# A decoder layer on one core: the order of the expert loads of a lane, and the sums of the conv norm moved to VectorE

## The chip, the cores and the metric

The kernel runs on one core of one Trainium2 chip. The metric is the device time of one execution in microseconds (us). A difference counts from about 0.5% of it, some 4.4 us.

## What is computed

One decoder layer for 512 tokens of width 1024, in 32-bit floats. The first half mixes tokens, the second half sends each token to two of 16 experts:

```python
h = _modulate(_rmsnorm(x, norm_mix_g[l]), sh1, sc1)
proj = h @ w_in                       # 1024 x 7168: q, fz, i, og, ca, cb, gate_a, gate_b
o = _hgrn2_chunkwise(q, k, v, log_f)  # 8 heads
y_a = (_rmsnorm(o, onorm_g) * silu(og)) @ w_o_hgrn
u = conv(ca * sigmoid(cb)) + conv_b   # 512 channels, 31 taps
u = jax.nn.silu(_layernorm(u, ln_g, ln_b))     # over the 512 channels
y_b = u @ w_o_conv
x = x + g1 * ((sigmoid(gate_a) * y_a + sigmoid(gate_b) * y_b) @ w_out)
for e in range(N_EXPERTS):            # group-limited top 2
    a = silu(hf @ w_gate[e]) * (hf @ w_up[e])
    y = y + comb[:, e:e + 1] * (a @ w_down[e])
```

## The kernel before

**Mixer.** `plan()` lists the weight chunks of 1 MB in the order in which TensorE uses them: cb, ca, then for each half of the heads (qd = 0, 1) fz, q, iv, og, then gb, yb, pairs of ga and ya, and wo. Each chunk has two tiles of output (yb: four), and tiles are numbered 0 to 79. A tile is 24 matmuls (yb: 12), since each 32-bit product is made of three (`mm3`, L555 to L557) from operands split into a high and a low part. The high part `w_hi` of a chunk is made by ScalarE (L939), the low part `w_lo` by VectorE (L1183), for chunk 24 by GpSimd (L1758, `POOL_SPLITS`); SyncE loads chunk n when the low part of chunk n-2 is done (L478). All engines walk the same list of tiles; between the tiles they do what `SLOT` puts behind a tile, each engine its own part, in program order.

Around the change these are tiles 40 to 47 (gb, evacuated by ScalarE into `mb`), 48 to 55 (yb, chunks 24 and 25, evacuated by VectorE) and 56 on (ga, ya). Behind tiles 40 to 44 come the last five steps x1 to x5 of the HGRN branch: transposes, state updates, outputs, mean squares (L700) and the spread of their inverse roots (L706, which waits for the reciprocal L1402 of VectorE). Then VectorE norms the heads (`o_norm`, L1432), GpSimd multiplies each with its gate (L1789), ScalarE and VectorE split it (L1029, L1437).

**Conv norm.** The conv has its result `acc` (4 channel tiles of 128 x 512) before tile 40. Its norm is four steps `("ln", 0..3)`, behind tiles 40 to 43. In step 0 TensorE forms the mean over the channels (L716, four matmuls of true 32-bit operands with `mean_c`), VectorE subtracts it (L1405), ScalarE squares (L1057). In step 1 TensorE forms the mean of the squares, again four matmuls, ScalarE takes the root (L1061), VectorE the reciprocal (L1410) and four products (L1413). In step 2 ScalarE makes the sigmoid (L1065), VectorE gain and bias (L1417) and the product (L1421). In step 3 ScalarE writes `cs_hi` (L1073) and VectorE `cs_lo` (L1425). Tile 48 is the first that reads them. After `cs_lo` GpSimd sets `ada_acc` to zero (L1792, at tile 44); SyncE waits for that between the loads of chunks 25 and 26 to load a bias row into it (L495). Loads of `ada_p` by ScalarE's queue and sums by VectorE (L1451, `ada_half`) follow from tile 50 on.

**Router.** VectorE makes the table of jobs. A job is 64 tokens of one expert; there are 24 jobs here. Three lanes (0, 1, 2) each have buffers for one expert, six pieces of 1 MB: 0 and 1 gate, 2 and 3 up, 4 and 5 down. Job j runs in round r = j // 3, lane j % 3. `jobs_i` says which expert a lane has in a round. The routing of these inputs gives lane 0 the experts 0 5 5 6 6 6 7 7, lane 1 15 down to 8, lane 2 1 1 2 3 4 4 4 4 in rounds 0 to 7: 13 of the 21 entries of rounds 1 to 7 need a load, 8 keep the expert.

**Expert loop.** For a job TensorE does in order: gate (pieces 0, 1; L856), the transposes of the job before (L878), up (2, 3; L856), the tokens of the next job (L846), down of the job before (4, 5; L892). Tokens come by a gather (GpSimd, L1805), results go by a scatter (L1816). SyncE refills the lanes; per round:

```python
for s, cs in ((0, (0, 1, 2, 3)), (1, (0, 1, 2, 3)), (0, (4, 5)), (2, (0, 1, 2, 3)), (1, (4, 5)), (2, (4, 5))):
    with sp.If(now[s] == old[s]):
```

Before each piece it waits until TensorE has released it. For a kept expert it loads 16 numbers in place of the piece, so that the count of the piece's semaphore goes on.

Of the kernel before, what the change touches and what calls it, by code (L numbers as in the profile page):

```python
# [92 lines left out]
def trunk_kernel(nc, xT, x, cols, consts, masks, w_ada, b_ada_row, w_in, w_o_hgrn, w_o_conv,  # L93
# [15 lines left out]
    with ctx:  # L109
# [177 lines left out]
        s_cz = sem("conv_silu_done")  # L287
        s_l1 = sem("ln_pe")
# [109 lines left out]
        for n in range(4):  # L398
            place(40 + n, ("ln", n))
# [66 lines left out]
        def _(sp):  # L466
# [60 lines left out]

            with sp.Fori(1, last + 1) as r:
                now = [sp.value_load(jobs_i[0:1, bass.ds(r + MAXR * s, 1)], min_val=0, max_val=NE - 1) for s in range(LANES)]
                old = [sp.value_load(jobs_i[0:1, bass.ds(r + (MAXR * s - 1), 1)], min_val=0, max_val=NE - 1) for s in range(LANES)]  # L530

                for s, cs in ((0, (0, 1, 2, 3)), (1, (0, 1, 2, 3)), (0, (4, 5)), (2, (0, 1, 2, 3)), (1, (4, 5)), (2, (4, 5))):
                    with sp.If(now[s] == old[s]):
                        for c in cs:
                            sp.wait_ge(s_gt if c < 2 else s_up if c < 4 else s_dn, r * LANES + (s - LANES + 1))
                            expert_load(sp, now[s], s, c, 16)
                    with sp.Else():
                        for c in cs:
                            sp.wait_ge(s_gt if c < 2 else s_up if c < 4 else s_dn, r * LANES + (s - LANES + 1))
                            expert_load(sp, now[s], s, c)  # L540
# [11 lines left out]
        def _(pe):  # L552
# [179 lines left out]
            for s, (kind, tile, n, t) in enumerate(steps):  # L732
# [148 lines left out]
            def down(j, r, s, first=False):  # L881
# [3 lines left out]
                for c in (4, 5):  # L885
                    pe.wait_ge(s_er[s][c], r * 16 + 16)
# [1004 lines left out]
```

## Time and profile before

| | us |
|---|---|
| median of 3 runs | 884.56 (883.62 to 887.65) |
| the profiled execution | 884.96 |
| its span, first to last instruction | 883.1 |
| TensorE busy | 819.2 |
| VectorE busy | 474.3 |
| ScalarE busy | 202.1 |
| GpSimd busy | 142.8 |

The granted clock of TensorE is the share of its full 2.4 GHz; it was 0.981 in the mean. A line such as L716 is a line of the kernel before. An idle time in brackets names what ended it. In the timelines consecutive instructions of one line stand in one row with their count.

### The profile page before, as it was taken

The numbers are of one execution on the slowest core, as the hardware profiler recorded it, in microseconds if no ns is written. First come the engines' busy times: TensorE is split into PE (matmuls) and PEld (weight loads), VectorE is DVE, ScalarE is ACT, GpSimd is POOL, SyncE is SP. The second block draws the span as 40 slices with busy tenths as digits, with TensorE's granted clock in tenths as the row PEclk, the third lists the DMA queues.
The fourth block names the chain that finished last, engine by engine and source line by source line (L and its number), as shares of the span: only waits on it lengthen the run. The fifth ranks groups of instructions, "written<-read, shape, count | busy, mean of one in ns | idle before, by whom it ended". The sixth has DMA issues, their size and how long they took to land.

```text
span 883.1 us, 14349 instructions
## 1 busy us (share of the span) xinstructions
PE 819.2 (93%) x5760; PEld 597.9 (68%) x5760; DVE 474.3 (54%) x634; ACT 202.1 (23%) x261; POOL 142.8 (16%) x200
## 2 busy tenths in 40 slices
PE   2999999999999999999999999799999889999960
PEld 0578889888799878778888898555555445555530
DVE  3659997995789956878777364611111101111117
ACT  3442211223321136412222523110000000000012
POOL 0000312220413200600000000022222212222220
PEclk9999999999999999999999999999999999999995
DMA  9922221212121211467774949996999999899316
GB/s 317 369 68 95 95 96 50 95 50 95 48 96 50 97 48 48 142 208 249 243 245 152 354 147 392 383 388 241 360 398 392 400 387 401 307 393 334 134 34 276
DMA packets 102303, 191.59 MB, mean 217 GB/s; under 512 B 4247, under 2 KB 41383, under 8 KB 102257
## 3 DMA queue, kind: packets, MB, share of 16 engines
q1 hardware_dynamic: 89138, 160.79, 50.4%
q10 hardware_dynamic: 9168, 19.40, 6.5%
q0 software_dynamic: 3952, 10.76, 3.3%
q8 instruction: 33, 0.54, 0.3%
q14 instruction: 12, 0.10, 0.0%
HBM read 182.55 MB, written 10.49 MB: 219 GB/s over the span
## 4 chain that ended last, share of the span: by engine, by line
PE 81%; DVE 7%; DMA 4%; SPq 4%; issue 2%; ACT 2%; POOL 0%; ACTq 0%; DVEq 0%; POOLq 0%
PE proj L856 16%; PE proj L555 15%; PE proj L557 14%; PE proj L556 14%; PE ha L892 8%; SPq L456 3%; PE pp L661 2%; PE pp L846 1%; DMA ew<-in_w_gate 1%; DMA xt_t<-in_xT 1%; PE ha L569 1%; PE ha L878 1%; PE ha L691 1%; PE pp L639 1%; PE pp L716 1%
## 5 line engine op out<-in xcount | busy, mean ns | idle before, releaser
L856 PE MATMUL proj<-ew,heT 128*64 128x256 f32 x1536 | 177.0, 383 | 5.9 <-DMA ew<-in_w_gate 3.8
L856 PEld LDWEIGHTS proj<-ew,heT 128*64 128x64 f32 x1536 | 109.5, 138 | 72.0 <-issue 17.8
L555 PE MATMUL proj<-h_hi,w_hi 128*128 128x512 f32 x368 | 146.2, 397 | 3.5 <-DVE h_lo L1224 3.0
L557 PE MATMUL proj<-h_hi,w_lo 128*128 128x512 f32 x368 | 143.4, 390 | 0.0
L556 PE MATMUL proj<-h_lo,w_hi 128*128 128x512 f32 x368 | 143.4, 390 | 0.0
L1346 DVE SCALAR_TENSOR_TENSOR acc<-u_t,cols_t,acc 128x512 f32<-128x512 f32 x120 | 91.1, 807 | 0.6
L892 PE MATMUL ha<-ew,aT 128*64 128x512 f32 x384 | 87.9, 599 | 1.8 <-DVE aT L1693 0.9
L1183 DVE TENSOR_TENSOR w_lo<-w_raw,w_hi 128x2048 fp32r<-128x2048 f32 x35 | 80.2, 2290 | 15.7 <-ACT w_hi L939 15.7
L939 ACT ACTIVATE w_hi<-w_raw 128x2048 fp32r<-128x2048 f32 x36 | 68.7, 1909 | 69.6 <-PE proj L557 44.8
L555 PEld LDWEIGHTS proj<-h_hi,w_hi 128*128 128x128 f32 x368 | 69.1, 188 | 22.2 <-issue 8.1
L557 PEld LDWEIGHTS proj<-h_hi,w_lo 128*128 128x128 f32 x368 | 69.1, 188 | 14.6
L556 PEld LDWEIGHTS proj<-h_lo,w_hi 128*128 128x128 f32 x368 | 69.1, 188 | 14.1 <-issue 0.5
L1698 DVE TENSOR_TENSOR y_sb<-ha,rows 128x512 f32<-128x512 f32 x24 | 16.6, 692 | 92.0 <-PE ha L892 92.0
L1801 POOL COPY gi<-idx_g 128x1 int32 (+1 forms) x25 | 4.7, 188 | 332.5 <-DVE idx_g L1676 191.4
L892 PEld LDWEIGHTS ha<-ew,aT 128*64 128x64 f32 x384 | 25.5, 136 | 47.3 <-issue 45.9
L1687 DVE TENSOR_TENSOR a_t<-proj,sg_t 128x256 f32<-128x256 f32 x24 | 10.2, 425 | 80.0 <-PE proj L856 80.0
L1693 DVE COPY aT<-ha 128x256 f32<-128x256 f32 x24 | 10.2, 424 | 79.5 <-PE ha L878 79.5
L1451 DVE SCALAR_TENSOR_TENSOR ada_acc<-ada_p,cact,ada_acc 128x512 f32<-128x512 f32 x64 | 47.9, 751 | 3.0 <-DMA ada_p<-in_w_ada 1.2
L1116 ACT ACTIVATE sg_t<-proj 128x256 f32<-128x256 f32 x24 | 9.2, 385 | 157.3 <-PE proj L856 157.3
L1122 ACT ACTIVATE heT<-pp 128x512 f32<-128x512 f32 x25 | 14.9, 598 | 103.6 <-PE pp L846 103.6
L555 PE MATMUL proj<-w_hi,h_hi 128*128 128x256 f32 x128 | 38.2, 298 | 0.0
L557 PE MATMUL proj<-w_hi,h_lo 128*128 128x256 f32 x128 | 37.6, 294 | 0.0
(252 smaller groups left out, 1233.0 us busy)
## 6 DMA issues: line engine op xcount, KB each, us to landing
ew<-in_w_gate SPq DMA_DIRECT2D x32, 1024.0 KB
ew<-in_w_up SPq DMA_DIRECT2D x32, 1024.0 KB, 14.9
ew<-in_w_down SPq DMA_DIRECT2D x32, 1024.0 KB
w_raw<-in_w_in SPq DMA_DIRECT2D x28, 1024.0 KB, 5.0
ada_p<-in_w_ada ACTq DMA_DIRECT2D x16, 1024.0 KB, 5.1
ada_w<-in_w_ada SPq DMA_DIRECT2D x8, 1024.0 KB, 13.4
w_raw<-in_w_o_hgrn SPq DMA_DIRECT2D x4, 1024.0 KB, 5.3
w_raw<-in_w_out SPq DMA_DIRECT2D x4, 1024.0 KB, 9.9
```

The lines of the kernel that those rows point to most:

```text
L456: eng.dma_start(dst, src).then_inc(s_er[s][c], 16)
L555: pe.matmul(outap, a_hi, b_hi, start=first, stop=False)
L556: pe.matmul(outap, a_hi, b_lo, start=False, stop=False)
L557: return pe.matmul(outap, a_lo, b_hi, start=False, stop=last)
L661: mm = pe.matmul(pp[64 * j:64 * j + keys, 32 * u:32 * u + 32], k_t[:, h, t0:t0 + keys], tblk(q_t[:, h, t0:t0 + 64], m, 1), start=True, sto ...
L856: mm = pe.matmul(out_ps[JS * i:JS * i + JS, 0:FG], heT[:, c_, JS * j_:JS * j_ + JS], w[:, k, FG * i:FG * i + FG], start=(kb == 0), stop=(k ...
L892: mm = pe.matmul(ha[JS * i:JS * i + JS, 1, 0:DG_], aT[:, c_, JS * i_:JS * i_ + JS], w[:, k, DG_ * i:DG_ * i + DG_], start=(fb == 0), stop= ...
L939: act.activation(w_hi[:, n % 2, :], w_raw[:, n % 2, :], ACT.Copy).then_inc(s_hi, 1)
L1183: dve.tensor_tensor(w_lo[:, n % 2, :], w_raw[:, n % 2, :], w_hi[:, n % 2, :].bitcast(F32), ALU.subtract).then_inc(s_lo, 1)
L1346: dve.scalar_tensor_tensor(acc[:, ct, :], src, tap, acc[:, ct, :], ALU.mult, ALU.add).then_inc(s_cv, 1)
L1451: dve.scalar_tensor_tensor(dst, ada_p[g % 2][:, k, :], cact[:, kk:kk + 1], dst, ALU.mult, ALU.add).then_inc(s_aa, 1)
L1698: dve.tensor_tensor(y_sb[:, :], ha[:, 1, 0:DG_], rows[:, 3, 0:DG_], ALU.mult).then_inc(s_y, 1)
```

## The change

1. Conv norm: VectorE adds the four channel tiles of `acc`, and later of the squares, in two steps each (128 x 1024, then 128 x 512) into `usq`, and TensorE needs one matmul for each mean in place of four. The steps stand behind tiles 40 (sum), 41, 42 (sum of squares), 44, 45 and 46 in place of 40 to 43; GpSimd's zeroing moves from tile 44 to 46.
2. Expert loads: SyncE refills in the order lane 0 pieces 0 to 3, lane 2 pieces 4 and 5 of the round before, lane 1 pieces 0 to 3, lane 0 pieces 4 and 5, lane 2 pieces 0 to 3, lane 1 pieces 4 and 5. The last pieces 4 and 5 of lane 2 come behind the loop.
3. A kept expert is marked in the table by VectorE, by 16 added to its number. For it SyncE raises the semaphore itself and loads nothing. Lane 2's pieces 4 and 5 get one more such step in round 0.
4. Three small matmuls are put in front of the wait for the first job's places.

```diff
+KEPT = NE
-        for n in range(4):
-            place(40 + n, ("ln", n))
+        for s0, what in ((40, "sum"), (41, 0), (42, "squares"), (44, 1), (45, 2), (46, 3)):
+            place(s0, ("ln", what))
...
+            def refill(s, cs, code, r):
+                done = [s_gt, s_gt, s_up, s_up, s_dn, s_dn]
+                with sp.If(code < KEPT):
+                    for c in cs:
+                        sp.wait_ge(done[c], r * LANES + (s - LANES + 1))
+                        expert_load(sp, code % NE, s, c)
+                with sp.Else():
+                    for c in cs:
+                        if s == 2 and c >= 4:
+                            sp.wait_ge(s_gt, r * LANES + 2)
+                        else:
+                            sp.wait_ge(done[c], r * LANES + (s - LANES + 1))
+                        sp.sem_inc(s_er[s][c], 16)
             with sp.Fori(1, last + 1) as r:
...
+                now = [entry(r, 0), entry(r, 1), entry(r, 2), entry(r - 1, 2)]
+                refill(0, (0, 1, 2, 3), now[0], r)
+                refill(2, (4, 5), now[3], r - 1)
+                refill(1, (0, 1, 2, 3), now[1], r)
+                refill(0, (4, 5), now[0], r)
+                refill(2, (0, 1, 2, 3), now[2], r)
+                refill(1, (4, 5), now[1], r)
+            refill(2, (4, 5), entry(last, 2), last)
...
             def layernorm_part(n):
+                pe.wait_ge(s_l0, 2 * n + 2)
...
-                for ct in range(CT):
-                    mm = pe.matmul(pp[:, 512 * n:512 * n + 512], mean_c, (usq if n else acc)[:, ct, :],
-                                   start=(ct == 0), stop=(ct == CT - 1))
+                mm = pe.matmul(pp[:, 512 * n:512 * n + 512], mean_c, usq[:, 0, :], start=True, stop=True)
...
+            busy(ha[:, 3, :], 3)
             pe.wait_ge(s_p1, 1)
...
-                    pe.wait_ge(s_er[s][c], r * 16 + 16)
+                    pe.wait_ge(s_er[s][c], r * 16 + (32 if s == 2 else 16))
...
+                    dve.tensor_tensor(usq[:, 0:2, :], src[:, 0:2, :], src[:, 2:4, :], ALU.add).then_inc(s_l0, 1)
+                    dve.wait_ge(s_l0, n + 1)
+                    dve.tensor_tensor(usq[:, 0, :], usq[:, 0, :], usq[:, 1, :], ALU.add).then_inc(s_l0, 1)
...
+            go(dve.memset(kept, 1.0))
...
-            go(dve.tensor_scalar(jobs_i[:, 0:NPOS], rt[:, 12, 0:NPOS], -1.0, None, ALU.add))
+            tt_(by_lane(kept)[:, :, 1:MAXR], by_lane(rt[:, 12, 0:NPOS])[:, :, 1:MAXR], by_lane(rt[:, 12, 0:NPOS])[:, :, 0:MAXR - 1],
+                ALU.is_equal)
+            settle()
+            go(dve.scalar_tensor_tensor(kept, kept, float(KEPT), rt[:, 12, 0:NPOS], ALU.mult, ALU.add))
+            settle()
+            go(dve.tensor_scalar(jobs_i[:, 0:NPOS], kept, -1.0, None, ALU.add))
...
-                if s == 44:
+                if s == 46:
                     pool.wait_ge(s_cl, CT)
                     pool.memset(ada_acc[:, :, :], 0.0).then_inc(s_az, 1)
```

VectorE in the kernel before, from the reciprocal of the conv norm to the split of chunk 25 (`acc` and `cs_lo` are the conv norm's, `o_t` and `on_lo` the heads'):

```order
L1410 RECIPROCAL rst<-rst 128x512
L1413 TENSOR_TENSOR acc<-acc,rst 128x512 x4
L1183 TENSOR_TENSOR w_lo<-w_raw,w_hi 128x2048
L1417 TENSOR_SCALAR acc<-acc,cols_t 128x512 x4
L1421 TENSOR_TENSOR acc<-acc,usq 128x512 x4
L1402 RECIPROCAL osq<-osq 128x512
L1425 TENSOR_TENSOR cs_lo<-acc,cs_hi 128x512 x4
L1183 TENSOR_TENSOR w_lo<-w_raw,w_hi 128x2048
L1432 SCALAR_TENSOR_TENSOR o_t<-o_t,cols_t,ha 128x512 x3
L1437 TENSOR_TENSOR on_lo<-o_t,on_hi 128x512 x2
L1432 SCALAR_TENSOR_TENSOR o_t<-o_t,cols_t,ha 128x512
L1437 TENSOR_TENSOR on_lo<-o_t,on_hi 128x512
```

VectorE in the changed kernel, the same stretch:

```order
L1436 RECIPROCAL rst<-rst 128x512
L1439 TENSOR_TENSOR acc<-acc,rst 128x512 x4
L1458 SCALAR_TENSOR_TENSOR o_t<-o_t,cols_t,ha 128x512 x2
L1443 TENSOR_SCALAR acc<-acc,cols_t 128x512 x4
L1447 TENSOR_TENSOR acc<-acc,usq 128x512 x4
L1458 SCALAR_TENSOR_TENSOR o_t<-o_t,cols_t,ha 128x512
L1463 TENSOR_TENSOR on_lo<-o_t,on_hi 128x512 x2
L1451 TENSOR_TENSOR cs_lo<-acc,cs_hi 128x512 x4
L1458 SCALAR_TENSOR_TENSOR o_t<-o_t,cols_t,ha 128x512
L1463 TENSOR_TENSOR on_lo<-o_t,on_hi 128x512
L1199 TENSOR_TENSOR w_lo<-w_raw,w_hi 128x2048
L1305 TENSOR_TENSOR mb_93<-proj,mb_93 128x512
```

The conv norm's low parts (`cs_lo`) stood ahead of everything of the heads; now they stand behind three steps of the heads' norm and behind two of the heads' low parts, and the products of step 2 stand directly before them.

GpSimd in the kernel before, in the same stretch (`k_t` is the last level of the scores, `spacer` belongs to the expert loop):

```order
L1785 TENSOR_TENSOR k_t<-k_t,tot_70 128x16x64
L1792 MEMSET ada_acc 128x4096
L1789 TENSOR_TENSOR o_t<-o_t,og_t 128x512 x2
L1758 TENSOR_TENSOR w_lo<-w_raw,w_hi 128x2048
L1789 TENSOR_TENSOR o_t<-o_t,og_t 128x512 x2
L1820 TENSOR_TENSOR spacer_128<-con_t 128x1
```

GpSimd in the changed kernel:

```order
L1819 TENSOR_TENSOR k_t<-k_t,tot_70 128x16x64
L1823 TENSOR_TENSOR o_t<-o_t,og_t 128x512 x2
L1792 TENSOR_TENSOR w_lo<-w_raw,w_hi 128x2048
L1823 TENSOR_TENSOR o_t<-o_t,og_t 128x512
L1826 MEMSET ada_acc 128x4096
L1823 TENSOR_TENSOR o_t<-o_t,og_t 128x512
L1854 TENSOR_TENSOR spacer_128<-con_t 128x1
```

The zeroing of `ada_acc`, which waits for `cs_lo`, moved from before all four gate products to between the third and the fourth, behind the split of chunk 24.

SyncE in the kernel before, at the top of a round (both branches of an If stand one behind the other):

```order
L530 TENSOR_LOAD jobs_i
L530 ISA x2
L533 COMPARE_AND_BRANCH
L535 ISA
L456 ISA
L456 DMA ew_0_131<-in_w_gate 1x16
L456 ISA
L456 DMA ew_1_132<-in_w_gate 1x16
L456 DMA ew_2_133<-in_w_up 1x16
L456 DMA ew_3_134<-in_w_up 1x16
L533 UNCONDITIONAL_BRANCH
L539 ISA
```

SyncE in the changed kernel:

```order
L532 TENSOR_LOAD jobs_i
L532 ISA x2
L537 COMPARE_AND_BRANCH
L539 ISA
L458 ISA
L458 DMA ew_0_131<-in_w_gate 128x4x512
L458 ISA
L458 DMA ew_1_132<-in_w_gate 128x4x512
L458 DMA ew_2_133<-in_w_up 128x4x512
L458 DMA ew_3_134<-in_w_up 128x4x512
L537 UNCONDITIONAL_BRANCH
L546 ISA
```

The small loads of a kept expert are gone; four table reads instead of six stand ahead of a round's first branch.

## Rows read from the trace of the kernel before

**Rows 1.** The page of the profile: busy time of the engines over the whole span.
```profile
PE 819.2 (93%) x5760; PEld 597.9 (68%) x5760; DVE 474.3 (54%) x634; ACT 202.1 (23%) x261; POOL 142.8 (16%) x200
```

**Rows 2.** The chain of waits, 310 to 332 us: start us, us, what ran.
```profile
317.50 3.44 PE pp L716 x8
...
329.10 3.44 PE pp L716 x8
```

**Rows 3.** TensorE's timeline, around 357 and 395 us (start, us, ..., [idle before]).
```profile
357.05 1.14 PE L706 MATMUL ha<-osq,con_t 32*128 32x512 f32 x8 [0.69 <-DVE osq L1402]
...
395.40 0.50 PE L555 MATMUL proj<-cs_hi,w_hi 128*128 128x512 f32 x1 [1.30 <-DVE mb L1289]
```

**Rows 4.** Busy time by stretch; per engine us (x instructions), PEclk, DMA share, GB/s.
```profile
410.00:460.00 50.00, 50.00 (x222) 41.40 (x222) 38.36 (x46) 14.12 (x14) 0.00 (x0) 1.00 0.73 242
```

**Rows 5.** VectorE's timeline, 333 to 371 us.
```profile
333.30 3.35 DVE L1410 RECIPROCAL rst<-rst 128x512 f32<-128x512 f32 x1 [0.57 <-ACT rst L1061]
...
351.24 2.49 DVE L1421 TENSOR_TENSOR acc<-acc,usq 128x512 f32<-128x512 f32 x4
...
356.91 2.43 DVE L1425 TENSOR_TENSOR cs_lo<-acc,cs_hi 128x512 fp32r<-128x512 f32 x4
...
366.89 4.68 DVE L1437 TENSOR_TENSOR on_lo<-o_t,on_hi 128x512 fp32r<-128x512 f32 x1 [3.37 <-ACT on_hi L1029]
```

**Rows 6.** ScalarE's timeline, 347 to 366 us.
```profile
347.82 2.93 ACT L1065 ACTIVATE usq<-acc,cols_t 128x512 f32<-128x512 f32 x4
...
364.43 1.91 ACT L939 ACTIVATE w_hi<-w_raw 128x2048 fp32r<-128x2048 f32 x1
```

**Rows 7.** GpSimd's timeline, 359 to 371 us.
```profile
359.40 3.53 POOL L1792 MEMSET ada_acc<- 128x4096 f32 x1 [46.88 <-DVE cs_lo L1425]
...
362.89 2.55 POOL L1789 TENSOR_TENSOR o_t<-o_t,og_t 128x512 f32<-128x512 f32 x2
...
366.42 4.61 POOL L1758 TENSOR_TENSOR w_lo<-w_raw,w_hi 128x2048 fp32r<-128x2048 f32 x1 [0.98 <-ACT w_hi L939]
```

**Rows 8.** TensorE's timeline in the expert loop, 679 to 726 us.
```profile
679.08 3.62 PE L856 MATMUL proj<-ew,heT 128*64 128x256 f32 x32
...
690.68 3.62 PE L856 MATMUL proj<-ew,heT 128*64 128x256 f32 x32
...
709.17 5.36 PE L856 MATMUL proj<-ew,heT 128*64 128x256 f32 x32 [3.83 <-DMA ew<-in_w_gate]
...
722.51 3.62 PE L856 MATMUL proj<-ew,heT 128*64 128x256 f32 x32
```

**Rows 9.** Who waited for whom, TensorE: us in total, times, longest.
```profile
PE proj L856 <- DMA ew<-in_w_up: 1.4, 2, 1.0
...
PE ha L892 <- DMA ew<-in_w_down: 0.9, 2, 0.5
...
PE pp L846 <- DMA xg<-h_rows,gi: 1.6, 1, 1.6
```

**Rows 10.** SyncE's DMA issues in the expert loop (start, us to issue, ...).
```profile
617.57 0.98 SPq L456 DMA_DIRECT2D ew<-in_w_gate  x2
...
697.42 0.72 SPq L456 DMA_DIRECT2D ew<-in_w_gate  x2
...
719.56 4.85 SPq L456 DMA_DIRECT2D ew<-in_w_down  x2
```

**Rows 11.** Busy time by stretch, columns as in rows 4.
```profile
610.00:615.00 5.00, 5.00 (x48) 3.07 (x46) 0.91 (x2) 0.39 (x1) 1.22 (x2) 1.00 0.14 52
...
710.00:715.00 5.00, 5.00 (x32) 2.73 (x30) 0.00 (x0) 0.39 (x1) 0.00 (x0) 0.66 1.05 390
```

**Rows 12.** Expert loads issued 699 to 757 us: time to landing.
```profile
DMA to landing us min/median/max: 16.6/16.9/17.3
```

**Rows 13.** The chain of waits, 742 us.
```profile
742.29 3.58 PE ha L892 x16
```

**Rows 14.** DMA issues of the page: count, KB each, median us to landing.
```profile
w_raw<-in_w_in SPq DMA_DIRECT2D x28, 1024.0 KB, 5.0
```

More of the change, by code:

```diff
@@ L287, in trunk_kernel @@
         s_cz = sem("conv_silu_done")
+        s_l0 = sem("ln_channel_tiles_added")
         s_l1 = sem("ln_pe")
@@ L526, in _, with entry @@
             last = last_round(sp)
-            with sp.Fori(1, last + 1) as r:
[L529 to L540, printed above, removed]
+            def entry(r, s):
+                return sp.value_load(jobs_i[0:1, bass.ds(r + MAXR * s, 1)], min_val=0, max_val=KEPT + NE - 1)
+            def refill(s, cs, code, r):
[11 more added lines that the diff above has]
+                        sp.sem_inc(s_er[s][c], 16)
+            with sp.Fori(1, last + 1) as r:
+                now = [entry(r, 0), entry(r, 1), entry(r, 2), entry(r - 1, 2)]
[6 more added lines that the diff above has]
+            refill(2, (4, 5), entry(last, 2), last)
             sp.wait_ge(s_ys, last * (16 * LANES) + (16 * LANES + 16))
@@ L768, in _ @@
                     elif what[0] == "ln":
-                        if what[1] < 2:
+                        if what[1] in (0, 1):
                             layernorm_part(what[1])
@@ L1056, in item @@
                     act.wait_ge(s_ld, 1)
+                    act.wait_ge(s_l1, 1)
                     act.activation(usq[:, :, :], acc[:, :, :], ACT.Square).then_inc(s_la, 1)
@@ L1402, in item @@
                     dve.reciprocal(osq[:, 0, :], osq[:, 0, :]).then_inc(s_ri, 1)
+                elif what[0] == "ln" and what[1] in ("sum", "squares"):
+                    n = 2 * (what[1] == "squares")
+                    src = usq if n else acc
+                    if n:
+                        dve.wait_ge(s_la, 1)
+                    else:
+                        dve.wait_ge(s_cv, CW * CT)
+                    dve.tensor_tensor(usq[:, 0:2, :], src[:, 0:2, :], src[:, 2:4, :], ALU.add).then_inc(s_l0, 1)
+                    dve.wait_ge(s_l0, n + 1)
+                    dve.tensor_tensor(usq[:, 0, :], usq[:, 0, :], usq[:, 1, :], ALU.add).then_inc(s_l0, 1)
                 elif what == ("ln", 0):
@@ L1520, in _ @@
                 dve.tensor_copy(lgt[:, P * tt:P * tt + P], logit_ps[tt]).then_inc(s_lc, 1)
+            kept = rt[:, 19, 16:16 + NPOS]
             go(dve.memset(r(19, 0, 16), 0.0))
+            go(dve.memset(kept, 1.0))
             dve.wait_ge(s_ys, 16)
```

4 lines of the change are left out of this document (1 added, 3 removed).

## The prediction, made before the changed kernel had run

> **What bounds the kernel now.** I read the page first: TensorE is busy 819 of 883 us [rows 1], so a step counts only if it stands on TensorE's path or makes TensorE wait. The chain of waits says which steps do. The conv norm's two means stand on it with 3.44 us each [rows 2]; TensorE has no gap around them. TensorE's timeline shows two small gaps in the same region: 0.69 us before the spread of the roots, where VectorE's reciprocal is late, and 1.30 us before tile 55, where VectorE is late again [rows 3]. In the expert loop a job takes 11.60 us (679.08 to 690.68), but the two after it together take 31.83 (690.68 to 722.51), so 8.63 us are lost there [rows 8], and the list of waits names the expert loads [rows 8, 9]. These are the places that the change touches.
>
> **Part 1, the conv norm on TensorE.** Eight true 32-bit matmuls become two: 6 x 3.44 / 4 = 5.2 us less [rows 2]. ScalarE and VectorE no longer have norm work in tiles 42 and 43 ahead of the root and reciprocal of the heads, so the 0.69 us go too [rows 3]. The four added sums on VectorE lie beside tiles 41 and 43, with the means needed a tile later: nothing. Tile 48 can then start 5.9 us earlier. Before, it started at about 374.5: the spread of roots issues from 357.05 to 358.1, and three tiles of 24 matmuls at 50/220 = 0.227 us follow [rows 3, 4]. So it could now start at 368.6.
>
> **What is late next.** Tile 48 needs `cs_lo`, and the chain to it starts later than before. Counted from 352.2 (three tiles before 368.6), where the second mean is ready: root 0.8 to 353.0, reciprocal 3.4 to 356.4, four products 2.5 to 358.9 (as the four of 2.49), two head norms, about 0.65 each, to 360.2, four gain steps, about 0.6 each, to 362.5 [rows 5]. ScalarE meanwhile ends tile 45's evacuation at 358.3, four sigmoids (2.93) at 361.2, the high part of chunk 24 (1.91) at 363.1 [rows 6]. That releases GpSimd's low part of chunk 24, 4.61 us [rows 7], just when VectorE is at its four products. And the trace has a row for what happens then: `on_lo`, a step of two SBUF inputs for which the like steps of `cs_lo` take 2.43/4 = 0.61 us, was issued at 366.89, 0.47 us after that same split of GpSimd had begun, and took 4.68 us, until just after the split's end at 371.03 [rows 5, 7]. So I let VectorE stand still: two products to 363.7, GpSimd 363.7 to 368.3, two products and a head norm to 370.2, two `on_lo` with a gate product of GpSimd (2.55/2 [rows 7]) between them to 372.7, the first `cs_lo` at 373.3. TensorE waits 4.7 us, and tile 48 starts 1.2 us earlier than before rather than 5.9.
>
> The Trainium skill ("SBUF — State Buffer", section "Who interferes with whom") states this as a rule against this change: a VectorE instruction with two SBUF inputs and a GpSimd instruction that reads SBUF exclude each other for a whole instruction. By it the sum is the one made here; without it tile 48 would keep its 5.9 us. The row of 4.68 us agrees with it.
>
> From tile 48 to tile 55 VectorE sets the pace as before (20.9 us from 374.5 to 395.40 [rows 3]), so nothing more is won or lost by order. But a gap of 4.7 us is longer than the 3.83 us that stood before the expert matmuls at 709.17; there the granted clock fell to 0.66 in the mean of 710 to 715, and 32 matmuls took 5.36 instead of 3.62 us, 1.74 more [rows 8, 11]. I take the same loss, of which waits for VectorE hide some 0.4: 1.3 us. **Part 1 in sum: -1.2 + 1.3, about 0.** Its ends: -5.9 if VectorE is not held, +2 if the second low part and the zeroing slip one more us each.
>
> The zeroing of `ada_acc` now ends at about 378.7 (last `cs_lo` 375.1, then 3.53 [rows 7]), and the load of chunk 26 is queued behind it on SyncE, as is the fourth gate product on GpSimd. The load lands 5.0 us after its issue [rows 14], at 384; ScalarE splits that chunk when tile 51 has ended, at about 386. Cover: 2 us.
>
> **Part 2, the router.** VectorE gets two small steps and their waits ahead of the table of gather indices. The first gather is waited for by TensorE for 1.6 us [rows 9], so their time is on the path; steps of this size follow each other at some 0.2 us, so +0.4. The four table reads instead of six start SyncE's first load about 1 us earlier, over the gather's tail. From both sides: 0 to +1.2, and I take +0.5. The mark's memset and the three small matmuls lie in waits for the router: nothing, by the same rows at most 0.3 either way.
>
> **Part 3, the expert loads.** The 8.63 us have two causes. The larger is a false wait. Job 12 keeps its expert; its 16-number load was issued at 697.42 and TensorE waited for it until 709.17, 11.75 us, since it stood in the queues behind 1 MB pieces [rows 8, 10]. With the semaphore raised by SyncE the wait of 3.83 us and the clock's loss of 1.74 us after it go: 5.57. The other 3.06 us (8.63 - 5.57) is real lateness: up and down pieces that landed late (1.4 + 0.9 us of waits, the rest lies between them [rows 9]).
>
> The Trainium skill ("DMA: Bandwidth & Descriptors", section "Anatomy of one DMA — SWDGE (gpsimd) path") gives a small DMA a fixed cost of about 2.0 us. By that alone the small load would have landed at 699.4, there would be no false wait, and part 3 would be worth 3 us at most. The row of 11.75 us decides against it here.
>
> For the real lateness look at when DMA had nothing to do: 0.14 of it busy from 610 to 615 [rows 11]. The pieces of job 7 were issued at 617.57 [rows 10], after the small ones and six table reads behind lane 2's down pieces, but TensorE had released them at the end of job 4's gate: 679.08 - 6 x 11.60 + 3.6 = 613.1. In the new order SyncE stands ready by then, so the queue starts 4.4 us earlier and, being full from there on, delivers everything 4.4 us earlier. That is more than 3.06, so the waits vanish. Later pieces have to come up to 8.6 us earlier and gain 4.4: the tightest is the second down piece of lane 1 in round 4. The two were issued in 719.56 to 724.4 [rows 10]; with 16.9 us to landing [rows 12] it was there at about 740.4, and used at 742.29 + 3.58/2 = 744.1 [rows 13]: 3.7 us of room, less 8.6 - 4.4 = 4.2. So at most 0.5 us returns; by the first piece, 2.7 us of room stay. **Part 3: -8.6**, ends -8.6 and -5.0.
>
> **Sum.** 0 + 0.5 - 8.6 = -8.1 us. The profiled execution took 884.96 us, 1.9 more than its span; the median is 884.56, within 0.4. I take it from the median: **876.5 us**. About 0.5%, 4.4 us, is what a measurement of this kernel can tell from no change.
>
> **Rivals.**
> A. *VectorE is not held.* If the high part of chunk 24 comes later, or GpSimd's split finds its place between VectorE's steps, part 1 is worth 5.9 us: -14.0, **870.6 us**. For it: some us of drift in ScalarE's order would do. Against: the row of 4.68 us, and that the split is needed by everything behind it.
> B. *Only the false wait goes.* The queue does not start earlier, or the order of pieces gives the 4.4 us back: the 3.06 us stay. -8.1 + 3.1 = -5.0, **879.6 us**. For it: DMA was full for over 100 us behind 620. Against: the idle stretch before it.
> C. *Slower.* The zeroing holds SyncE's queue, and the loads of chunks 26 and 27 run beside those of `ada_p` and take 11.75 us, as an expert-loop load did, in place of 5.0 [rows 10, 14]. Each is then 6.75 us late; the first has 2 us of cover, the second none: +11.5 - 8.1 = +3.4, **888.0 us**. It decides once a chunk takes more than 7 us to land. Against: DMA is not full there.
> D. *The marks fail*, so that kept experts are loaded again: 48 pieces of 1 MB at 390 GB/s, 2.7 us each, 129 us more, **1006 us**. Nothing in the code speaks for it.
>
> **How the numbers follow.** Forecast 0.62, A 0.20, B 0.15, C 0.02, D 0.01. The range takes in A (870.6) and B with 0.2 beyond each, since the small ends of parts 1 and 2 lie inside: 870.4 to 879.8; outside it are C, D and tails, within 2 in 10. No change begins at 880.1 us: half of B and a sliver of the forecast's tail reach it with the scatter of the runs: same 0.09. Faster 0.88, slower 0.03.
>
> **What would show it.** L716's successor twice with 0.86 us; a gap of TensorE of 4 to 5 us before tile 48, ended by `cs_lo`; a step of VectorE of over 4 us while GpSimd splits chunk 24; clock below 1 around 373 to 377. In the loop: 11.60 us for every job from the second on, no wait for an expert load above 0.5 us, no small loads, clock 1.00 throughout, and the first piece of job 7 issued within 0.3 us of the end of job 4's gate. No gap before tile 48 would prove part 1 wrong, a gap at job 11 or 12 part 3.

## The result: 879.94 us, 0.58% faster, and the profile after

Six executions of the changed kernel took 879.45 to 881.91 us, median **879.94 us**; six of the kernel before on the same chip had a median of 885.50 us. The ratio is 0.9942 with a 95% interval of 0.9926 to 0.9958: faster by 0.58%. The forecast was 876.5 us with a range up to 879.8; the time lies just above it. The profiled execution took 879.63 us, its span is 877.8 us (before 883.1).

The page of the profile after, busy times and the clock in 40 slices:
```profile
PE 816.4 (93%) x5754; PEld 598.0 (68%) x5754; DVE 479.0 (55%) x641; ACT 202.1 (23%) x261; POOL 147.1 (17%) x200
...
PEclk9999999999999999989999999999999999999995
```
TensorE has 6 instructions and 2.8 us less, GpSimd is busy 4.3 us longer with the same 200 instructions [rows 1], and slice 18, around 373 to 395 us, has a lower clock that it did not have before.

I cut both traces at three instructions that both kernels have. **Stretch 1** goes from the last decay-level group before the norm's region (twelve `ha<-con_t,k_t`) to tile 55, behind the idle 1.30 us [rows 3]; it holds part 1. **Stretch 2** goes from job 0's gate to the start of the last down and holds part 3 and most of part 2. TensorE's timeline after, the rows at these cuts and at the waits between them (start, us, ..., [idle before]):
```profile
315.66 1.47 PE L691 MATMUL ha<-con_t,k_t 128*128 128x128 f32 x12
...
372.87 0.77 PE L573 MATMUL proj<-cs_hi,w_hi 128*128 128x512 f32 x1 [4.37 <-DVE cs_lo L1451]
...
381.61 0.50 PE L573 MATMUL proj<-cs_hi,w_hi 128*128 128x512 f32 x1 [0.51 <-DVE mb L1305]
...
396.82 0.50 PE L573 MATMUL proj<-cs_hi,w_hi 128*128 128x512 f32 x1 [1.30 <-DVE mb L1305]
...
565.97 7.13 PE L871 MATMUL proj<-ew,heT 128*64 128x256 f32 x64
574.96 0.66 PE L861 MATMUL pp<-con_t,xg 128*128 128x128 f32 x4 [1.85 <-DMA xg<-h_rows,gi]
576.30 5.31 PE L871 MATMUL proj<-ew,heT 128*64 128x256 f32 x32 [0.69 <-ACT heT L1138]
...
601.18 3.62 PE L871 MATMUL proj<-ew,heT 128*64 128x256 f32 x32
...
846.25 3.65 PE L907 MATMUL ha<-ew,aT 128*64 128x512 f32 x16 [0.93 <-DVE aT L1727]
```
The same cuts in the kernel before, same view:
```profile
316.03 1.47 PE L673 MATMUL ha<-con_t,k_t 128*128 128x128 f32 x12
...
574.63 3.67 PE L856 MATMUL proj<-ew,heT 128*64 128x256 f32 x32 [0.69 <-ACT heT L1122]
...
597.88 2.33 PE L856 MATMUL proj<-ew,heT 128*64 128x256 f32 x20
...
851.58 3.65 PE L892 MATMUL ha<-ew,aT 128*64 128x512 f32 x16 [0.93 <-DVE aT L1693]
```
Job 0's gate started at 564.56 before. So:

| stretch | before | after | difference |
|---|---|---|---|
| to the level group | 316.03 | 315.66 | -0.4 |
| 1: level group to tile 55 | 79.37 | 81.16 | **+1.8** |
| tile 55 to job 0's gate | 169.16 | 169.15 | 0.0 |
| 2: job 0's gate to the last down | 287.02 | 280.28 | **-6.7** |
| last down to the end | 31.54 | 31.55 | 0.0 |

They add up to the 5.3 us between the spans. From the gate of job 3 (597.88 before, 601.18 after) to the last down it is 253.70 against 245.07: 8.63 us less, the part 3 of the forecast. TensorE's matmuls after wait for no expert load at all [rows 9], every job takes 11.60 us, and the first pieces of job 7 are issued 0.6 us after the end of job 4's gate (601.18 + 11.60 + 3.6 = 616.4). SyncE's issues after:
```profile
616.97 0.94 SPq L458 DMA_DIRECT2D ew<-in_w_gate  x2
```
What is new are two stretches of lower clock. Busy time by stretch after, columns as in [rows 4] (0.57 means that most of the window ran at 1.2 instead of 2.4 GHz):
```profile
371.00:379.00 8.00, 6.13 (x16) 4.87 (x17) 5.23 (x9) 2.92 (x3) 7.93 (x2) 0.57 0.00 0
...
576.00:580.00 4.00, 3.70 (x20) 2.17 (x22) 0.00 (x0) 0.24 (x1) 1.13 (x2) 0.57 1.02 375
```
and the two windows of the kernel before: at 576 the full clock, at 710 the drop behind the false wait, which is gone after.
```profile
576.00:580.00 4.00, 4.00 (x38) 2.44 (x36) 0.42 (x1) 0.39 (x1) 0.00 (x0) 1.00 1.04 392
710.00:714.00 4.00, 4.00 (x26) 2.29 (x24) 0.00 (x0) 0.00 (x0) 0.00 (x0) 0.57 1.05 389
```
By the clock's own record the drop of the norm lasts from 371.43 to 378.26 us, 6.83 us, twice the 3.41 us of the one at 710; the one at the router from 576.23 to 579.64.

Now the region of the norm on the other engines after. VectorE's timeline:
```profile
360.02 7.83 DVE L1443 TENSOR_SCALAR acc<-acc,cols_t 128x512 f32<-128x512 f32 x4
367.78 2.48 DVE L1447 TENSOR_TENSOR acc<-acc,usq 128x512 f32<-128x512 f32 x4
...
372.05 2.49 DVE L1451 TENSOR_TENSOR cs_lo<-acc,cs_hi 128x512 fp32r<-128x512 f32 x4
...
376.37 0.69 DVE L1463 TENSOR_TENSOR on_lo<-o_t,on_hi 128x512 fp32r<-128x512 f32 x1 [1.18 <-ACT on_hi L1044]
378.66 2.29 DVE L1199 TENSOR_TENSOR w_lo<-w_raw,w_hi 128x2048 fp32r<-128x2048 f32 x1 [1.59 <-ACT w_hi L954]
380.86 0.69 DVE L1305 TENSOR_TENSOR mb<-proj,mb 128x512 f32<-128x512 f32 x1
```
GpSimd's:
```profile
362.96 4.61 POOL L1792 TENSOR_TENSOR w_lo<-w_raw,w_hi 128x2048 fp32r<-128x2048 f32 x1 [0.63 <-ACT w_hi L954]
371.07 4.61 POOL L1823 TENSOR_TENSOR o_t<-o_t,og_t 128x512 f32<-128x512 f32 x1 [3.49 <-DVE o_t L1458]
375.62 3.52 POOL L1826 MEMSET ada_acc<- 128x4096 f32 x1
379.09 2.99 POOL L1823 TENSOR_TENSOR o_t<-o_t,og_t 128x512 f32<-128x512 f32 x1
```
ScalarE's:
```profile
375.71 0.63 ACT L1044 ACTIVATE on_hi<-o_t 128x512 fp32r<-128x512 f32 x1 [4.78 <-POOL o_t L1823]
...
376.72 1.90 ACT L954 ACTIVATE w_hi<-w_raw 128x2048 fp32r<-128x2048 f32 x1
```
The reader is to see two engines that hold each other, in turn. While GpSimd splits chunk 24 (362.96 to 367.57), VectorE's gain steps stand: four take 7.83 us, where four products take 2.48. The longest single one took 4.87 us (durations in ns, min/median/max):
```profile
L1443 DVE TENSOR_SCALAR acc<-acc,cols_t x4: 535/1336/4865, 360.0 to 363.0; 128x512 f32<-128x512 f32 x4
```
And then, while VectorE runs seven steps back to back, GpSimd's gate product of the third head takes 4.61 us, where two of them took 2.55 before [rows 7]. Behind that product a chain goes through all engines: `on_hi` 375.71, the high part of chunk 25 at 376.72, its low part at 378.66, the eviction of tile 48 at 380.86, and TensorE waits for the last at 381.61. The forecast had the first hold, not the second.

### The profile page after: what moved, and what is told of

The parts are those of the page before. It is cut to its first block, busy times and chain, and to the rows that moved or that the text cites. A ratio compares the mean times of both kernels' runs of the same rounds, so it can differ in the third digit from the quotient of the medians.

```text
span 877.8 us, 14227 instructions
## 1 busy us (share of the span) xinstructions
PE 816.4 (93%) x5754; PEld 598.0 (68%) x5754; DVE 479.0 (55%) x641; ACT 202.1 (23%) x261; POOL 147.1 (17%) x200
## 4 chain that ended last, share of the span: by engine, by line
PE 84%; DVE 8%; DMA 3%; issue 2%; ACT 2%; POOL 1%; SPq 0%; ACTq 0%; DVEq 0%; POOLq 0%
PE proj L871 19%; PE proj L573 15%; PE proj L575 14%; PE proj L574 14%; PE ha L907 10%; PE pp L679 2%; PE pp L861 2%; DMA xt_t<-in_xT 1%; PE ha L893 1%; PE ha L587 1%; DVE acc L1443 1%; PE ha L709 1%; PE pp L657 1%; PE ha L742 1%; DVE rt L1535 1%
## 5 line engine op out<-in xcount | busy, mean ns | idle before, releaser
L574 PE MATMUL proj<-w_lo,h_hi 128*128 128x256 f32 x128 | 37.6, 293 | 0.0
## 6 DMA issues: line engine op xcount, KB each, us to landing
ada_w<-in_w_ada SPq DMA_DIRECT2D x8, 1024.0 KB, 13.5
```

What stands on the lines that cost most here:

```text
L574: pe.matmul(outap, a_hi, b_lo, start=False, stop=False)
```

## The experiments

Each ratio below is to the kernel before on the same chip. Fillers are small matmuls put ahead of a wait, with their sums thrown away. Stretches are read from one profiled execution of each kernel. The whole times scatter more than in the first comparison (the kernel before alone from 883.5 to 891.4 us on one chip), since lower clock comes and goes in code that no version touches: the level group starts between 315.54 and 320.55 us, with 6.8 to 17.1 us of lower clock ahead of it. So the verdicts go by stretches 1 and 2 of the profiled execution; where kernels share the code of a stretch and its clock, the traces agree within 0.1 us (79.37, 79.32, 79.31, 79.32 for the old norm; 81.16, 81.14, 81.14 for the new).

| kernel | whole us, ratio (interval) | stretch 1 (lower clock in it) | stretch 2 (lower clock) |
|---|---|---|---|
| before | | 79.37 (0) | 287.02 (3.41) |
| changed | 879.94, 0.9942 (0.9926-0.9958) | 81.16 (6.83) | 280.28 (3.41) |
| 1 norm only | 887.67, 1.0018 (0.9998-1.0037) | 81.14 (6.83) | 285.02 (0) |
| 2 without the norm | 879.27, 0.9907 (0.9874-0.9940) | 79.32 (0) | 281.67 (6.83) |
| 3 split on VectorE | 879.08, 0.9911 (0.9880-0.9942) | 79.02 (3.41) | 281.83 (6.83) |
| 4 norm one tile earlier | 878.32, 0.9899 (0.9868-0.9929) | 79.34 (0) | 280.13 (3.41) |
| 5 fillers, tile 48 | 881.51, 0.9951 (0.9930-0.9973) | 81.19 (0) | 280.25 (3.41) |
| 6 fillers, both places | 879.74, 0.9924 (0.9902-0.9945) | 81.17 (0) | 278.65 (0) |
| 7 marks alone | 882.41, 0.9944 (0.9923-0.9965) | 79.31 (0) | 283.11 (6.83) |
| 8 order alone | 880.99, 0.9942 (0.9926-0.9959) | 81.14 (6.83) | 280.16 (3.41) |
| 9 product on VectorE | 880.41, 0.9925 (0.9903-0.9947) | 81.10 (6.83) | 278.30 (0) |
| 10 product and fillers | 878.16, 0.9902 (0.9882-0.9922) | 79.00 (0) | 278.85 (0) |
| 11 as 2, with fillers | 877.35, 0.9891 (0.9873-0.9910) | 79.32 (0) | 278.69 (0) |
| 12 as 3 and 4 together | 874.73, **0.9872** (0.9850-0.9894) | **77.20** (0) | 278.56 (0) |

Stretch 2 with the new order of loads comes in three sizes, by lower clock alone: 278.3 to 278.9 without, 280.1 to 280.3 with 3.41 us, 281.7 to 281.8 with 6.83 us. One drop of 3.41 us costs 1.6 us there. The whole times that experiments 3, 4 and 6 expected (877, 877.5 and 875 us at most) did not come.

**1. The conv norm's part alone**, with its sums, waits and the zeroing, in the kernel before; of its edit the steps' places:
```diff
-        for n in range(4):
-            place(40 + n, ("ln", n))
+        for s0, what in ((40, "sum"), (41, 0), (42, "squares"), (44, 1), (45, 2), (46, 3)):
+            place(s0, ("ln", what))
...
-                if s == 44:
+                if s == 46:
                     pool.wait_ge(s_cl, CT)
```


> The kernel before with the conv norm's part alone (sums on VectorE, the steps at tiles 40 to 46, the zeroing at 46). Theory T (read from the trace after): the 4.4 us wait of TensorE before tile 48 comes back, the clock falls to its lower level behind it, and tile 55 starts about 1.4 us later than in the kernel before; everything behind is the old program shifted. In all 1.4 slower (886.0 to 887.5), up to 1.7 more if the shift also brings the second clock drop at the router. Forecast's own sum: 0. If VectorE were not held (rival A): 5.9 faster. A drop shorter than 5 us of lower clock would speak against T.


Measured: 887.67 us (ratio 1.0018), the interval just includes no change. The wait before tile 48 is 4.38 us, the drop 6.83 us, stretch 1 takes 81.14 us: 1.8 longer than before. Part 1 costs time by itself. The false wait is there, but 3.27 us long in place of 3.83, and no drop follows it: the matmuls behind it run at full clock.
```profile
559.72 5.33 PE L823 MATMUL pp<-h_t,place 128*64 128x512 f32 x16 [0.79 <-DVE place L1596]
...
711.59 3.67 PE L853 MATMUL proj<-ew,heT 128*64 128x256 f32 x32 [3.27 <-DMA ew<-in_w_gate]
```
Instead a drop stands at 559.7 us, in the router as it was before (5.33 us for 16 matmuls that take 3.65 at full clock).

**2. Without the conv norm's part** (all four steps at tiles 40 to 43, eight mean matmuls, zeroing at 44; the rest as changed).


> The changed kernel with the conv norm as before (all four steps at tiles 40 to 43, eight mean matmuls). Theory T: the loads' part is worth 8.6 and the two added steps of the router cost 0.3, so 885.5 - 8.3 = 877.2, if the second clock drop, at 576 us, came from the new position in time that part 1 gave the router; if that drop belongs to the router's own change, 878.9. Against T: 879.9 or slower, which would say that part 1 costs nothing.


Measured: 879.27 us, with single executions near 876.3 (two, mean clock 0.982), near 881.0 (three, 0.976 to 0.977) and one at 877.6 (0.980). Stretch 1 is that of before. The profiled execution is one of those near 881.0 and has 6.83 us of lower clock from 575.5 on, behind a wait of 1.93 us for the gather, so the drop does not need part 1.

**3. Chunk 24's low part on VectorE.**
```diff
-        POOL_SPLITS = [steps[at_step[z]][2] + 1 for z in (("gb", 6),)]
+        POOL_SPLITS = []
```


> The changed kernel with the low part of chunk 24 formed on VectorE instead of GpSimd. Theory T (VectorE's gain and bias steps are held by GpSimd's 4.61 us step): the gain step falls from 4.87 us to about 2, VectorE gets one 2.4 us step more, TensorE's wait before tile 48 shrinks from 4.4 us to under 2.5 and the clock stays up: 3 to 5 faster than the changed kernel (875 to 877). Rival (VectorE has simply too much to do there, whoever splits): the wait stays at 4 us or more, and the time within 1 us of the changed kernel's 879.9.


VectorE's timeline here:
```profile
361.38 3.50 DVE L1443 TENSOR_SCALAR acc<-acc,cols_t 128x512 f32<-128x512 f32 x4
...
367.21 2.28 DVE L1199 TENSOR_TENSOR w_lo<-w_raw,w_hi 128x2048 fp32r<-128x2048 f32 x1
```
Without the split on GpSimd the four gain steps take 3.50 us in place of 7.83 (two gate products of GpSimd still run beside them); the wait is 2.25 us, the drop 3.41 us, stretch 1 is 2.1 us shorter. So the hold by the split made some half of the 4.37 us of wait, and 2.25 us stay without it. That the clock would stay up was wrong. The second hold is there without any split: GpSimd's gate product of the third head, beside the same seven steps of VectorE,
```profile
370.30 4.61 POOL L1823 TENSOR_TENSOR o_t<-o_t,og_t 128x512 f32<-128x512 f32 x1 [6.61 <-DVE o_t L1458]
```

**4. The norm's last steps one tile earlier.**
```diff
-        for s0, what in ((40, "sum"), (41, 0), (42, "squares"), (44, 1), (45, 2), (46, 3)):
+        for s0, what in ((40, "sum"), (41, 0), (42, "squares"), (43, 1), (44, 2), (45, 3)):
```


> The changed kernel with the last three steps of the conv norm at tiles 43, 44, 45, so that VectorE's gain and bias run before GpSimd's split at tile 46 begins. Theory T: gain and bias take their usual 2 us, the wait before tile 48 becomes under 2 us, the clock stays up: 875 to 877.5. Rival (the work of VectorE in tiles 43 to 48 is what is late, in whatever order): the wait moves to an earlier tile, the time stays at 879 to 881.


VectorE's and GpSimd's timelines here:
```profile
362.13 1.91 DVE L1443 TENSOR_SCALAR acc<-acc,cols_t 128x512 f32<-128x512 f32 x4
...
367.68 8.68 DVE L1451 TENSOR_TENSOR cs_lo<-acc,cs_hi 128x512 fp32r<-128x512 f32 x4
```
```profile
370.21 5.01 POOL L1792 TENSOR_TENSOR w_lo<-w_raw,w_hi 128x2048 fp32r<-128x2048 f32 x1
```
The gain steps take 1.91 us, as expected, and the split now holds `cs_lo`: 8.68 us for four. The hold moved. TensorE waits 1.82, 1.64 and 1.72 us before three tiles, in place of 4.37 once; the clock stays up, and stretch 1 is 1.8 us shorter than in the changed kernel and no shorter than before.

**5. Fillers ahead of tile 48.** The test of whether the lost microseconds of part 1 are the clock.
```diff
                         if kind == "yb":
                             if tile == 0:
+                                if k == 0:
+                                    busy(bank, 18)
                                 pe.wait_ge(s_cl, k + 1)
```


> The changed kernel with 18 small matmuls (128 columns each, their sums thrown away) in the bank of tile 48 ahead of the wait for the conv's output, so that TensorE is busy for some 3.9 of the 4.37 us for which it would wait. Nothing gets earlier by it. Theory T (the loss of part 1 against its forecast is the clock that falls behind that wait): the stretch from the last decay-level matmul of the first quad (ha<-con_t,k_t) to tile 55 takes 77.7 instead of 81.2 us and shows no lower clock; the whole is 3.4 less than the changed kernel wherever the other drops stay the same. Rival (tiles 48 to 55 are slow for data that come late, and the clock does not matter): the stretch stays at 81 us.


TensorE's timeline here, and busy time by stretch:
```profile
373.94 0.50 PE L573 MATMUL proj<-cs_hi,w_hi 128*128 128x512 f32 x1 [0.27 <-DVE cs_lo L1453]
...
378.04 0.50 PE L573 MATMUL proj<-cs_hi,w_hi 128*128 128x512 f32 x1 [1.09 <-ACT mb L1015]
...
382.78 0.50 PE L573 MATMUL proj<-cs_hi,w_hi 128*128 128x512 f32 x1 [1.72 <-DVE mb L1307]
```
```profile
371.00:379.00 8.00, 6.63 (x40) 5.47 (x40) 6.05 (x10) 3.21 (x5) 6.78 (x2) 1.00 0.00 0
```
The clock is 1.00, and nothing is gained: 81.19 us. The rival held. TensorE at full clock runs into waits of 1.09 and 1.72 us for evictions. My theory of this point (all of it is the clock) fell. The new one, tried in experiments 9 and 10: the chain behind GpSimd's held product is as late as the slow clock makes TensorE.

**6. Fillers there and in job 0's waits.**
```diff
                 up(j, r, s, first)
+                if first:
+                    busy(ha[:, 3, :], 8)
                 tokens(j + 1)
+                if first:
+                    busy(ha[:, 3, :], 3)
```


> As the one before, and 8 + 3 small matmuls also in the waits of 1.86 and 0.69 us behind job 0's up. Theory T (the drop at 576 us comes from those waits): the stretch from job 0's gate to the last down takes 278.6 us instead of 280.3, with no lower clock in it, and the whole comes to 875 or less. Rival (the drop comes from what lies ahead of job 0, the router's chain of short waits): the drop stays, 280.3 us or somewhat more for the fillers.


TensorE's timeline here:
```profile
578.06 3.67 PE L873 MATMUL proj<-ew,heT 128*64 128x256 f32 x32
```
Job 1's gate takes 3.67 us as before the change, in place of 5.31, and stretch 2 takes 278.65 us without lower clock. The drop at 576 came from the idle 1.85 + 0.69 us and costs 1.6 us.

**7. The marks alone, in the old order of pieces.**
```diff
                     with sp.If(now[s] == old[s]):
...
-                            expert_load(sp, now[s], s, c, 16)
+                            sp.sem_inc(s_er[s][c], 16)
```


> The kernel before with one edit: the kept job's pieces are marked by SyncE instead of loaded by a small transfer; the order of the pieces stays the old one. Theory T, by the three terms of the forecast: the wait of 3.83 us goes, the pieces that came really late stay late (3.06 us in waits of 0.3 to 1.0 us), the clock drop that stood behind the 3.83 goes or moves to another place. Stretch from job 0's gate to the last down: 287.0 - 3.8 = 283.2 us with one drop still in it, 281.5 without. Rival (the order is what counts, the marks nothing): 286 to 287 us.


Measured: 283.11 us with 6.83 us of lower clock. TensorE's matmuls here wait for no gate load any more and for no up piece (1.4 us before), and for the down pieces as before
```profile
PE ha L892 <- DMA ew<-in_w_down: 0.9, 2, 0.5
```
The expected 283.2 us came by luck, with two drops in place of one. Less 2 x 1.6 for the clock it is 279.9, only 1.2 us above the 278.7 of the new order; from the gate of job 3 to the last down it is 246.47 us, against 253.70 before and 245.07 after. So most of the 3.06 us of "real lateness" went as well, which I had not expected: TensorE came 3.3 us later to the loop by the drops at the router, which is time for the pieces; that this is the cause was not tried.

**8. The order alone, with the small transfers.**
```diff
                 with sp.Else():
                     for c in cs:
...
-                        sp.sem_inc(s_er[s][c], 16)
+                        expert_load(sp, code % NE, s, c, 16)
```


> The changed kernel with the kept job's small transfers put back in place of the marks; the new order stays. Theory T: the small transfer of job 11 again lands behind the large ones ahead of it in the queue; in the new order it has one piece less or more ahead of it, so the wait of 3.83 us stays within 2 of that, and only the 3.06 us of real lateness are gone: stretch from job 0's gate to the last down 282.5 to 284.5 us. Rival (in the new order the small ones are early enough): 280.3 us as in the changed kernel.


SyncE's issues and TensorE's timeline here:
```profile
691.88 0.73 SPq L458 DMA_DIRECT2D ew<-in_w_gate  x2
```
```profile
705.42 3.62 PE L870 MATMUL proj<-ew,heT 128*64 128x256 f32 x32
```
All of stretch 2 is that of the changed kernel (280.16 and 280.28), with no wait for an expert load. The rival held: the small transfer of job 12 (the expectation calls it job 11) is issued at 691.88, 5.5 us earlier than before [rows 10], and is there when its gate starts at 705.42, with 13.5 us in between where it had needed 11.75. The order is worth the whole gain; the marks add nothing to it that a trace shows.

**9. The third head's gate product on VectorE.** The new theory of experiment 5, by itself.
```diff
                                          ALU.mult, ALU.mult).then_inc(s_or, 1)
+                if (qd, h) == (1, 2):
...
+                    dve.tensor_tensor(o_t[:, h, :], o_t[:, h, :], og_t[:, h, :], ALU.mult).then_inc(s_oo, 1)
...
+                    if (qd, h) == (1, 2):
+                        continue
```


> The changed kernel with one gate product, that of head 2 of the second quad (4.61 us on GpSimd, while VectorE runs its steps back to back), computed on VectorE instead, some 0.7 us there. New theory U (after the experiment with fillers ahead of tile 48, where the clock stayed up and nothing was gained): tile 55's start hangs on that product, through ScalarE's queue behind it (head 2's high part, an eviction, chunk 25's high part), VectorE's low part of chunk 25 and tile 48's eviction. Then the chain ends some 3.5 us earlier, and now the lower clock behind the wait before tile 48 decides: stretch from the last level matmul to tile 55 about 80.0 to 80.7 us (changed kernel 81.2). Rival (the 4.61 us are beside other work): 81.2 or, with 0.7 more on VectorE, 81.9.


TensorE's timeline here:
```profile
374.01 0.77 PE L573 MATMUL proj<-cs_hi,w_hi 128*128 128x512 f32 x1 [5.16 <-DVE cs_lo L1451]
...
397.11 0.50 PE L573 MATMUL proj<-cs_hi,w_hi 128*128 128x512 f32 x1 [1.30 <-DVE mb L1305]
...
576.26 3.67 PE L871 MATMUL proj<-ew,heT 128*64 128x256 f32 x32 [0.69 <-ACT heT L1138]
```
Between tile 48 and tile 55 no wait is left. ScalarE makes the high part of chunk 25, which stood at 376.72 behind the held product, 3.6 us earlier:
```profile
373.11 1.90 ACT L954 ACTIVATE w_hi<-w_raw 128x2048 fp32r<-128x2048 f32 x1
```
So the product was what TensorE waited for at tile 50. The time stays at 81.10 us, above the 80.0 to 80.7 expected: the wait before tile 48 is 0.8 us longer, and the 6.83 us of lower clock are now felt. Job 1's gate takes 3.67 us here, with no drop at 576: the gather was waited for only 1.51 us.

**10. Both together.** The edits of 6 and 9.


> As the one before, with the fillers ahead of tile 48 and in job 0's two waits. Theory U: with the product off the path and the clock up, both limits of this stretch are gone: 77.8 to 78.8 us from the last level matmul to tile 55, and 278.6 from job 0's gate to the last down; as a whole 4 less than the changed kernel where the earlier stretch is equal. Rival (something else of VectorE or GpSimd is as late as the product): 80 us or more with the clock up.


TensorE's timeline here:
```profile
373.95 0.50 PE L573 MATMUL proj<-cs_hi,w_hi 128*128 128x512 f32 x1 [1.05 <-DVE cs_lo L1457]
...
395.04 0.50 PE L573 MATMUL proj<-cs_hi,w_hi 128*128 128x512 f32 x1 [1.29 <-DVE mb L1311]
```
Now the stretch falls, to 79.00 us, 0.2 above the range expected. The four versions are a square: neither edit 81.16, clock alone 81.19, product alone 81.10, both 79.00. Counted from tile 48 on they are 23.95, 24.06, 23.10 and 21.09: the late chain costs 3.0 us by itself, the lower clock 2.0, and both together no more than the longer of the two. The square is not quite clean: the product on VectorE makes tile 48 0.8 us later, and this takes back the 0.9 us that its move alone gains. Stretch 2 takes 278.85.

**11. Experiment 2 with the fillers of job 0.**


> Without the conv norm's part: the changed loads and router, and the 8 + 3 fillers in job 0's two waits. Every account so far: 79.3 us from the last level matmul to tile 55 and 278.6 from job 0's gate to the last down, no lower clock in either; 3.4 less than the changed kernel where the stretch ahead is equal, 876.5. Against it: a drop in either stretch.


Measured: 877.35 us, 79.32 and 278.69 us, no lower clock in either. Both stretches as expected, the whole 0.8 us above the 876.5 us expected.

**12. The edits of 3 and 4 together, with the fillers of job 0.**


> The changed kernel with chunk 24's low part on VectorE and the norm's last three steps at tiles 43 to 45, and the 8 + 3 fillers in job 0's waits. Each of the first two alone gave 79.0 and 79.3 us from the last level matmul to tile 55. Theory U: with no GpSimd split to hold VectorE's cs_lo steps (5.04 us for one in the version one tile earlier) the wait before tile 48 is under 1.5 us, no lower clock, 77.5 to 78.5 us. Rival (VectorE's own work in these tiles is the limit, whoever holds whom): 79 us again.


VectorE's timeline here:
```profile
357.12 1.91 DVE L1447 TENSOR_SCALAR acc<-acc,cols_t 128x512 f32<-128x512 f32 x4
...
362.67 4.32 DVE L1455 TENSOR_TENSOR cs_lo<-acc,cs_hi 128x512 fp32r<-128x512 f32 x4
```
TensorE's:
```profile
369.25 0.50 PE L573 MATMUL proj<-cs_hi,w_hi 128*128 128x512 f32 x1 [0.81 <-DVE w_lo L1203]
...
377.55 0.50 PE L573 MATMUL proj<-cs_hi,w_hi 128*128 128x512 f32 x1 [1.72 <-DVE mb L1309]
```
874.73 us, ratio 0.9872 (0.9850 to 0.9894): faster than both kernels, 1.3% below the kernel before. The sums on VectorE are worth 2.2 us against before once GpSimd no longer splits a chunk beside them and the norm's last steps stand a tile earlier. The `cs_lo` steps are held less, 4.32 us for four (two gate products of GpSimd run beside them) in place of 8.68. The 1.72 us for an eviction stay.

## Why the prediction was wrong, point by point

**Part 1, tile 48: right in size.** The forecast had VectorE held during GpSimd's split, a wait of 4.7 us and tile 48 at 373.3; it was 4.37 us and 372.87. The held steps were the gain steps and not the products; the split began at 362.96, 0.7 us before its forecast time. The Trainium skill ("SBUF — State Buffer", section "Who interferes with whom") gives the rule for VectorE steps with two SBUF inputs, and I used only that part of it. The gain step has one such input and its scalars. The same section lists `tensor_scalar`, the operation of the gain steps, among those that can enter a mode in which they, too, contend with GpSimd, under conditions that no run here tests. The trace agrees that it can be held: 4.87 us.

**Part 1, behind tile 48: the step that failed.** The text says "From tile 48 to tile 55 VectorE sets the pace as before (20.9 us ...), so nothing more is won or lost by order", and it counts GpSimd's gate product at 2.55/2 us. It was counted as a step that nobody holds, in a stretch where VectorE runs seven steps back to back. It took 4.61 us, and the stretch took 396.82 - 372.87 = 23.95 us in place of 20.9 + 1.3. I had applied the hold in one direction only. The +1.8 us for the whole part lies inside the end of +2 that the forecast gave it, but that end was reasoned from other steps.

**Part 1, the clock: mis-sized, too.** 1.3 us were taken from a drop of 3.41 us; this one lasted 6.83 us. By itself it makes this part 23.1 us (experiment 9: 397.11 - 374.01), 2.0 more than with the clock up (experiment 10: 21.09). The chain and the clock run in parallel, and the longer of them, the chain with 24.0 us, sets the time: the sum of part 1 was +1.8 instead of 0.

**Part 2: the two steps right, a drop missed.** The gather is issued 3.64 us behind the start of job 0's gate with the old router (before, experiment 7) and 4.09 to 4.11 us with the new one (all kernels that have it): 0.46 us more, where 0.4 was counted. The gather itself took 0.20 us less in the trace after, so that the wait for it grew only from 1.60 to 1.85 us, +0.26 from the gate's start to the tokens; the marks' memset and three matmuls cost nothing visible (tile 55 to job 0's gate is equal). But the 1.85 + 0.69 us were followed by a drop of the clock and 1.6 us more, where 1.60 + 0.69 were followed by none. I had looked for drops behind new waits only, not behind a wait of before that grows a little, and the range of this term, 0 to +1.2, was too narrow by that. In the traces without fillers the wait is 1.60, 1.52 and 1.98 us with the old router and 1.51 to 2.09 us with the new one: the gather itself scatters by more than the two steps add, and a drop of 6.83 us came with the old router too (experiment 7). So the drop is partly luck of the execution.

**Part 3: right in sum, wrong in its parts.** -8.63 us, with 11.60 us for every job and the queue starting at the release, as forecast. The working had two causes, the false wait (with its clock) removed by the marks, and the lateness removed by the order. The order alone removes both (experiment 8), since it also issues the small transfer 5.5 us earlier; the marks alone remove nearly as much. They are two cures for one trouble, and adding them happened to give the right sum. The 2.0 us that the forecast took from the Trainium skill ("DMA: Bandwidth & Descriptors", section "Anatomy of one DMA — SWDGE (gpsimd) path") are fitted there for the queue of GpSimd, and this load went by SyncE's; that the row of 11.75 us decides is not touched by it.

**The sum**: +1.8 + 0.3 + 1.6 - 8.6 = -4.9 us, with -0.4 us of difference ahead of the norm -5.3, against -8.1 forecast. Of the 3.2 us that are missing, 1.8 are part 1 and 1.4 part 2, where 1.6 us of drop were not counted and the rest was counted 0.2 too high.

**The rivals.** Rival B (879.6) named the time that came, but not the way: its mark, waits that stay in the expert loop, is absent. Rival A (VectorE not held) is refuted by the 4.37 us. Rival C needed SyncE's queue or late chunks: in stretch 1 no wait of TensorE names a DMA. Rival D did not occur.

## What to carry to other kernels

When work is moved to an engine that shares its time with another, count the hold in both directions: list every step of either that now meets a run of back-to-back steps of the other, and follow the held one to whom it releases. A clock drop and a late chain in the same stretch are parallel limits: test them in a square of four before giving either the blame, and look what the edit itself delays. And when two edits aim at the same wait, ask first whether each alone removes it; here reordering a queue did, and the marks came for nothing.

## What the runs showed of the hardware that I had not expected

- A step of VectorE with one SBUF tensor and per-partition scalars (gain and bias) was held 4.87 us by GpSimd's 4.61 us split; the four took 7.83 us, and 1.91 us where no GpSimd step ran.
- The hold works the other way as well: GpSimd's 128x512 product took 4.61 us while VectorE ran seven steps back to back, with a split on GpSimd just before (after) and with none (experiment 3); 1.60 in the version one tile earlier, and 1.29 where VectorE ran one step of 0.68 us beside it (experiment 10, the fourth product).
- Ahead of the last 25 to 28 us of the kernels lower clock came for 3.41 or 6.83 us at a time. At one place longer waits went with more of it; across places they did not order it. At job 0's waits, ten traces without fillers: none behind a wait for the gather of 1.51, 1.52 and 1.60 us, 3.41 us behind 1.67, 1.68, 1.77 and 1.85, 6.83 us behind 1.93, 1.98 and 2.09. Elsewhere: none behind 1.82, 1.64 and 1.72 us (experiment 4) and 3.27 us (experiment 1), 3.41 us behind 2.25 (experiment 3) and 3.83, and also in the router of experiment 1 behind only 0.79, 6.83 us behind 4.37, 4.38 and 5.16. Eleven small matmuls in the wait removed it in four of four kernels.
- It also came in code that is equal in all versions and has no wait of this kind named in its place, up to 17.1 us ahead of the level group (experiment 4). Why there is open.
